# Padding between the slots of two weight rings and around the normed activations

## The reference

```python
# first block, layer 0 (retention), layer 1 (latent attention)
h = rms_norm(x, pre_norm_g[i])
z = h @ w_in                      # 1024 x 6144, or 1024 x 3136
...                               # retention, or attention on 256 latent columns
y = (silu(gate) * o) @ w_out      # 2048 x 1024
x = x + rms_norm(y, post_norm_g[i])
x = x + (p[i] @ ple_w_proj[i]) * sigmoid(x @ ple_w_gate[i])
# second block
mod = silu(c) @ w_ada + b_ada     # 1024 x 6144, one row
proj = h @ w_in                   # 1024 x 3584
ya = silu(layer_norm(causal_dwconv(a_val * sigmoid(a_gate), w_dw_a))) @ w_pw_a
yb = causal_multiscale_pool(u_pool) @ w_pool
mix = (sigmoid(gate_a) * ya + sigmoid(gate_b) * yb) @ w_out
up = causal_dwconv(h @ w_up, w_dw_f)     # 1024 x 5632
f = (gelu(gt) * v) @ w_down              # 2816 x 1024
```

## Time and profile before

| | |
|---|---|
| median of 3 runs | 845.52 us (844.92 to 847.47) |
| the profiled execution | 846.33 us |
| its span, first to last instruction | 844.5 us |
| granted TensorE clock, mean | 0.997 |
| PE busy | 831.2 us (98%), 5434 matmuls |
| DVE busy | 667.9 us (79%) |
| ACT busy | 454.9 us (54%) |
| HBM read | 167.36 MB |

### The profile page before, as it was taken

One profiled execution on the slowest core, in us unless ns is written; L12 is line 12 of the kernel. 1 busy time (PEld: TensorE's weight loads), 2 busy tenths in 40 slices (PEclk: granted clock), 3 DMA queues, 4 the chain that ended last, 5 costly groups with the idle time before them and its releaser, 6 DMA issues.

```text
span 844.5 us, 15113 instructions
## 1 busy us (share of the span) xinstructions
PE 831.2 (98%) x5434; PEld 759.5 (90%) x5434; DVE 667.9 (79%) x982; ACT 454.9 (54%) x680; POOL 48.7 (6%) x61
## 2 busy tenths in 40 slices
PE   9999999999999999999999999999999999999995
PEld 9899999988878999999988889988988999999884
DVE  7979888686966887787866777999898888788566
ACT  6464545554646665657555536102853867777440
POOL 0009000000012000000000000060000000000000
PEclk9999999999999999999999999999999999999998
DMA  7857565679634747383648562444662565566541
GB/s 271 303 196 246 204 243 200 223 252 379 226 102 162 263 137 264 114 286 124 243 149 329 196 224 97 133 152 157 219 219 99 199 204 188 179 193 229 187 164 50
DMA packets 48141, 168.98 MB, mean 200 GB/s; under 512 B 5602, under 2 KB 6242, under 8 KB 48100
## 3 DMA queue, kind: packets, MB, share of 16 engines
q1 hardware_dynamic: 40324, 142.18, 49.6%
q10 hardware_dynamic: 7776, 26.25, 8.7%
HBM read 167.36 MB, written 1.05 MB: 199 GB/s over the span
## 4 chain that ended last, share of the span: by engine, by line
PE 85%; DVE 8%; issue 3%; ACT 2%; DMA 1%; DVEq 1%; ACTq 0%
PE bank L478 13%; PE bank L479 12%; PE bank L480 12%; PE bank L545 9%; PE bank L547 9%; PE bank L546 9%; DVE WK L1982 4%; PE bank L491 3%; PE bank L696 2%; PE bank L697 2%; PE bank L698 2%; PE bank L588 1%; DVE wlo L1495 1%; PE bank L819 1%; PE bank L837 1%
## 5 line engine op out<-in xcount | busy, mean ns | idle before, releaser
L971 ACT ACTIVATE whi<-raw 128x1024 fp32r<-128x1024 f32 (+1 forms) x232 | 240.1, 1040 | 218.3 <-PE bank L480 95.3
L1495 DVE TENSOR_TENSOR wlo<-raw,whi 128x1024 fp32r<-128x1024 f32 (+1 forms) x232 | 278.5, 1212 | 79.7 <-ACT whi L971 77.1
L478 PE MATMUL bank<-H,whi 128*128 128x256 f32 x784 | 224.5, 286 | 0.5 <-DVE wlo L1495 0.5
L480 PE MATMUL bank<-H,wlo 128*128 128x256 f32 x784 | 221.8, 283 | 0.0
L479 PE MATMUL bank<-H,whi 128*128 128x256 f32 x784 | 221.7, 283 | 0.0
L478 PEld LDWEIGHTS bank<-H,whi 128*128 128x128 f32 x784 | 150.3, 192 | 1.8 <-issue 1.7
L479 PEld LDWEIGHTS bank<-H,whi 128*128 128x128 f32 x784 | 150.4, 192 | 0.1
L480 PEld LDWEIGHTS bank<-H,wlo 128*128 128x128 f32 x784 | 150.3, 192 | 0.0
L545 PE MATMUL bank<-whi,Y 128*128 128x512 f32 x216 | 84.3, 390 | 0.0
L547 PE MATMUL bank<-whi,Y 128*128 128x512 f32 x216 | 84.1, 389 | 0.0
L546 PE MATMUL bank<-wlo,Y 128*128 128x512 f32 x216 | 84.1, 389 | 0.0
(11 more groups left out here) (275 smaller groups left out, 1362.8 us busy)
## 6 DMA issues: line engine op xcount, KB each, us to landing
ada_raw<-ada_in ACTq DMA_DIRECT2D x48, 512.0 KB, 4.4
raw<-w_head SPq DMA_DIRECT2D x47, 512.0 KB, 4.4
raw<-w_up SPq DMA_DIRECT2D x42, 512.0 KB, 3.3
raw<-w_down SPq DMA_DIRECT2D x22, 512.0 KB, 4.2
raw<-w_uq SPq DMA_DIRECT2D x24, 384.0 KB, 3.1
raw<-w_ret_out SPq DMA_DIRECT2D x16, 512.0 KB, 5.6
raw<-w_mla_gate SPq DMA_DIRECT2D x16, 512.0 KB, 4.5
raw<-w_mla_out SPq DMA_DIRECT2D x16, 512.0 KB, 5.1
```

The costliest lines, as they stand in the source:

```text
L478: mm(o, whi[:, s, c], a[:, 0, :], start=start, stop=False)
L480: last = mm(o, wlo[:, s, c], a[:, 0, :], start=False, stop=stop)
L971: activation(parts_of(b, n)[0], block_in(b, n), ACT.Copy).then_inc(hi_done, 1)
L1495: tt(lo, block_in(b, n), f32(hi), ALU.subtract).then_inc(lo_done, 1)
```

## The change

Each slot of `whi` and `wlo` gets 8 floats (32 bytes) in each partition behind it; the names `whi` and `wlo` become views that leave these out, so all uses of them stay as they are. Two tiles of 8 floats, which nothing reads or writes, are declared ahead of `H` and behind it. No instruction is added, removed or moved, and no shape of one changes.

```diff
         raw = sb("raw", [P, RING, 1024])
-        whi = sb("whi", [P, RING, 1024], F32R)
-        wlo = sb("wlo", [P, RING, 1024], F32R)
+        whi_padded = sb("whi", [P, RING, 1024 + 8], F32R)
+        wlo_padded = sb("wlo", [P, RING, 1024 + 8], F32R)
+        whi, wlo = whi_padded[:, :, 0:1024], wlo_padded[:, :, 0:1024]
         ada_raw = sb("ada_raw", [P, 2, 1024])
         ada_acc = sb("ada_acc", [P, 2, 1024])
         X = sb("X", [P, 2, D])
+        ahead_of_h = sb("ahead_of_h", [P, 8])
         H = sb("H", [P, DT, 2, T], F32R)
+        behind_h = sb("behind_h", [P, 8])
         Y = sb("Y", [P, FF_TILES, 2, T], F32R)
```

## The result

The changed kernel takes 847.21 us (median of 20 runs, 845.97 to 850.89), the kernel before 845.70 in as many (844.53 to 847.98): a ratio of 1.0018, interval 1.0010 to 1.0026. That is 1.5 us slower: less than the 0.3% (2.5 us) that the prediction counts as no effect, and clear of zero only by the number of runs. The forecast of 845.6 us and no change held. What stood behind it did not.

The account below looks back on a forecast made before the run. The prediction took PE, by the pace of its matmuls, as the bound. Operand displacement on PE, the ACT and DVE split and the DMAs were each taken as 0, sum 0, giving 845.6 us, range 842 to 849.

Parts of the forecast that it names:

- a collision that the padding relieves: Rival: PE's weight load and moving stream collide on one raster; padding gives back up to 43 us (802 us); chance 0.11.
- displaced slots that read worse: Rival: PE's weight load and moving stream meet at new distances, 8 ns on three quarters of 4320, 872 us; chance 0.10.
- the 4320: Matmuls with an operand in `whi`, `wlo` or `H`, or behind the padding: 3000 of 256 columns, 1320 of 512.
- Step (a): PE reading displaced slots and a displaced `H`: ends minus 43 us and plus 26 us, taken as 0.
- three readings: For no PE effect: starts steady under ACT's and DVE's writes, float32 trains unaffected by displacement, pace constant over differing operand distances.
- The trains of 32 in float32: Lines 615 and 491, 32 matmuls of 128 columns each: both 3.57 us, one operand off the raster or both on it.
- The bound of 43 us: Most that better addresses could give back on PE: 4320 matmuls at 10 ns each.
- the remainder above the float32 form: Some 10 ns in each of 4320 PE matmuls, independent of columns, that the float32 form doesn't show.
- the slower rival: Displaced slots read worse on PE: 8 ns on three quarters of 4320, 26 us, giving 872 us; chance 0.10.
- Step (b): ACT's copies (median 1060 ns) and DVE's subtractions (1221) in the weight split: 2.3 us either way beside PE, taken as 0.
- Step (c): DMAs into displaced tiles, `X` at the start: allowed 0.5 us either way, taken as 0.
- The rival that the padding is rounded away: Tiles placed on a raster coarser than 32 bytes, so only slots move; forecast time unchanged, chance within the 0.76 for no change.

Follow-up runs that it names:

- e2: Against the kernel before, only the tiles of 8 floats ahead of and behind `H` added, rings as before; 846.56 us, ratio 1.0006.
- e11: The kernel of e10 with no edit, traced a second time on another chip; 838.57 us in its one run, 846.58 for the kernel before beside it.
- e5: Against the kernel before, only `raw` moved by 32 bytes, with `whi`, `wlo`, `H`, `Y` and `S` kept on one raster; ratio 1.0000.
- e6: Against the kernel before, `H` placed 64 bytes and `Y` and `S` 192 bytes off the 512-byte raster, rings as before; 841.73 us against 845.74.
- e7: Against the kernel before, `H` placed 128 bytes and `Y` and `S` 256 bytes off the 512-byte raster, rings as before; ratio 0.9997.
- e1: Against the kernel before, only the slots of `whi` and `wlo` padded, no tiles around `H`; 845.15 us against 845.49, ratio 0.9988.
- e10: Against the kernel before, `H` 448 bytes off the raster, the latents in `Y` 192 through a view, the rest of `Y` on it; 837.77 us against 845.49.
- e9: Against the kernel before, `H` and the latents in `Y` (through a view) 192 bytes off the raster, the rest of `Y` on it; 839.59 us against 845.49.

## Why the prediction was right, and where it was not

**The time was right by luck: two effects cancel that I had put down as two rivals.** I gave 0.11 to a collision that the padding relieves and 0.10 to displaced slots that read worse. By their signs both happened, each in one form of the product: 3000 matmuls gain 2 ns, 1320 lose 5. I had treated the 4320 as one population, in which 0.6 ns would decide. By form, 2 x 3000 and 5 x 1320 are 6.0 and 6.6 us, each more than twice 0.3%, and nothing in the prediction made them equal.

**Step (a), "I take 0", is the one that failed.** It put the effect of the distance on PE's pace at nothing, where the runs show -2 ns and +5 ns. Its three readings were true and did not bear on the question. That ACT's and DVE's writes don't disturb PE holds in the displaced kernels as well (e2, e11), but the two streams that meet are PE's own. The trains of 32 in float32 speak for float32 only: they take 3.57 us in the changed kernel too, and the 256-column form of float32 is at 215.8 ns in the kernel before and in e2, e5 and e6, where its operands are 0, 64, 32 and 192 bytes apart. So the prediction's argument that a collision would hit the float32 form as well fails: that form doesn't answer to distance, the float32r form does. And that slots, parts and k differ in their distance modulo 1024 to 4096 while the pace is constant tests nothing if the pace repeats every 256 bytes, as e7 has it: every operand of the kernel before had distance 0. I had written that no row has a float32r product off the raster; that sentence deserved the weight which I gave to the readings beside it.

**The bound of 43 us was mis-sized.** I priced it at 10 ns for each of the 4320, the remainder above the float32 form. The best steady pace seen is 113.3 of 120 in the 256-column form, so 6.7 x 3000 = 20 us; the 512-column form has no steady pace under its 226.8 of before in any trace, so nothing there. The price of the slower rival came near by luck: 8 ns was the stretch of one duration of line 547, not a distance of starts, and the displaced 512-column form lost 5 ns in the changed kernel and 6.5 in e2.

**The rest of the steps held.** Step (b): ACT's and DVE's medians moved by 1 ns each (1061, 1222). Step (c): nothing later at the start; the first strip of `H` begins at 16.8 us, before at 17.6 (one execution of each). The rival that the padding is rounded away is out, since e1 and e2 each act.

**What I said would show the forecast wrong did show.** "120 ns apart" and "at 227" became 113 to 123 and 227 to 236 for nine of ten distances with `H`. By my own test the mechanism was refuted and only the sum survived. Of the measured 1.5 us the paces of the traced execution explain 0.6; the remaining 0.9 us stay open (the two traced executions themselves have one span, 844.5 us). A pace that a wait picks, as e10 and e11 show it for 448 bytes, and the clock at 600 us vary from execution to execution, but neither was traced often enough in the changed kernel to say.

**The two streams of PE.** The distance between the two operands of PE moves its pace by up to 6.7 ns in 120, and the other engines are ruled out (e5, and the pace under their writes). The page TensorE: Matmul & The Clock Gate of the Trainium skill, section "Step-by-step: what each phase is for", says that loading the next weights takes no read bandwidth from the running matmul. For float32r operands the pace depends on how the two lie to one another (120.0 or 113.3 ns), which that sentence alone would not lead one to expect; where the two differ, these runs decide. Why the operands act on each other (which part of the memory, which port) no run shows.

## What to carry to other kernels

Where PE is the bound, compare the distance of matmul starts by form with one another, and try the distance between the moving and the stationary operand modulo 256 bytes as a parameter: it costs a few hundred bytes and here, for float32r products, was worth 0.9% in a tuned kernel. Choose it for each form and each stage; one padding for all of them lost in one form what it won in the other. A constant pace over many addresses proves nothing while all of them are alike modulo the period, and a sum of zero can be two effects, so an experiment should be read by the stage and not by the time.

## What the runs showed of the hardware that I had not expected

- The pace of float32r matmuls on a distance of operands: 120.0 ns (256 columns) and 226.8 (512) at 0 bytes, the same means at 256, about 117 and 233 at 32, 118.9 and 232.4 as means at 128. The plain float32 form (256 columns) is at 215.8 ns at 0, 32, 64 and 192 bytes.
- At 64, 192 and 448 bytes there are two steady paces, 113.3 and 117.8 ns. One of them holds for hundreds of matmuls, and the next wait of PE, or the next matmuls of another form, may bring the other; two executions of one program, on two chips, differ in it over 40 blocks. The times spread too: six of e10, all on one chip, lie between 835.75 and 842.24 us, where eleven of the kernel before lie between 844.99 and 848.09. That the pace is what spreads them is likely and not shown, since only one of the six was traced. Whether a wait can be made to pick the fast one was not tried.
- Near 600 us PE waits for `G`. In the window from 590 to 630 us the granted clock was 0.96 in e5 (a wait of 2.0 us) and in e11 (1.7 us), and 1.00 in e9 (1.7 us as well), e10 (1.5 us) and before (1.0 us). The length of the wait alone doesn't decide it; what else does is open.
